# Attention run one stage deeper: scores three steps ahead, maxima two, division by the sums one, values one behind

## The reference

```python
# diff: 4 heads, two score maps each, shared values
a = masked_softmax(s1, mask) - lam * masked_softmax(s2, mask)
out = einsum('bhqk,bkhd->bqhd', a, v)
# fox: 8 heads; c is the cumulated log of the forget gate
s = einsum('bqhd,bkhd->bhqk', qb, k) * scale + cq[..., :, None] - c[..., None, :]
out = einsum('bhqk,bkhd->bqhd', masked_softmax(s, mask), v)
# nsa: 16 heads in 4 groups; compressed, selected and window keys
o = gb[:, :, 0] * o_c + gb[:, :, 1] * o_s + gb[:, :, 2] * o_w
```

## Time and profile before

| | before |
|---|---|
| median of 3 runs | 2183.83 us |
| profiled execution, time | 2185.85 us |
| profiled execution, span from first to last instruction | 2184.0 us |
| mean granted TensorE clock | 0.938 |
| busy: TensorE, VectorE, ScalarE, GpSimd | 1835.5, 638.7, 477.5, 461.3 us |
| attention, first scores to last output copy | 144 to 879 us |
| last fill ends | 787 us |

### The profile page before, as it was taken

The page is one execution under the profiler, slowest core; times in us unless marked ns, Lnnn a source line. Parts: engine busy times, 40 slices in busy tenths (PEclk is TensorE's granted clock), DMA queues, the critical chain, the costliest instruction groups (busy, mean ns, idle before and its releaser), DMA issues. The chain is left out here.

```text
span 2184.0 us, 27742 instructions
## 1 busy us (share of the span) xinstructions
PE 1835.5 (84%) x11130; PEld 1284.6 (59%) x11130; DVE 638.7 (29%) x1270; ACT 477.5 (22%) x1005; POOL 461.3 (21%) x340
## 2 busy tenths in 40 slices
PE   6999999999999977999748878888788888787870
PEld 4887777776666654888635545554455555454530
DVE  4433334436665577100321111111111111111115
ACT  4222323323434343222201010101010101010101
POOL 2333323332221120344121111111111111111100
PEclk9999999999999987999969999999999999999995
DMA  9552222332131120233539999999999999999966
GB/s 266 125 160 77 77 59 78 77 74 52 39 68 49 44 111 1 68 99 95 234 146 421 420 423 421 422 420 423 421 422 421 420 421 422 420 421 418 416 252 249
DMA packets 206614, 527.21 MB, mean 241 GB/s; under 512 B 65922, under 2 KB 149154, under 8 KB 162122
## 3 DMA queue, kind: packets, MB, share of 16 engines
q1 hardware_dynamic: 187738, 509.15, 61.2%
q0 software_dynamic: 18800, 17.00, 2.3%
HBM read 530.38 MB, written 46.03 MB: 264 GB/s over the span
## 5 line engine op out<-in xcount | busy, mean ns | idle before, releaser
L790 PE MATMUL PJ<-ht_rounded,ring_rounded 128*128 128x512 f32 (+1 forms) x928 | 322.7, 401 | 4.5 <-ACT at_region L1148 3.8
L1031 PE MATMUL PJ<-ht_region,ring_region 128*64 128x256 f32 x1024 | 254.7, 412 | 65.7 <-DMA ht_region<-in_w_up 65.7
L1031 PE MATMUL PJ<-at_region,ring_region 128*64 128x256 f32 x1024 | 243.2, 399 | 58.5 <-DMA at_region<-in_w_up 57.6
L1032 PE MATMUL PJ<-ht_region,ring_region 128*64 128x256 f32 x1024 | 255.4, 413 | 0.0
L1032 PE MATMUL PJ<-at_region,ring_region 128*64 128x256 f32 x1024 | 243.9, 399 | 0.0
L1031 PEld LDWEIGHTS PJ<-ht_region,ring_region 128*64 128x64 f32 x1024 | 150.2, 149 | 152.9 <-issue 96.5
L728 POOL DMA_INDIRECT y_scratch<-ring_region,s_idx x64 | 64.6, 1009 | 789.8 <-DVE ring_region L1653 765.2
L1031 PEld LDWEIGHTS PJ<-at_region,ring_region 128*64 128x64 f32 x1024 | 145.1, 144 | 139.9 <-issue 90.0
L676 POOL TENSOR_TENSOR ring_rounded<-ring_region,at_rounded 128x2048 fp32r<-128x2048 f32 (+1 forms) x31 | 139.7, 4505 | 346.3 <-ACT at_rounded L1093 346.3
L676 POOL TENSOR_TENSOR ring_rounded<-ring_region,ring_rounded 128x2048 fp32r<-128x2048 f32 x30 | 137.7, 4591 | 322.6 <-ACT ring_rounded L1093 322.6
L1645 DVE TENSOR_TENSOR ring_region<-ring_region,PJ 64x256 f32<-64x256 f32 x64 | 27.1, 423 | 603.6 <-ACT ring_region L1294 603.6
(11 more groups left out here) (242 smaller groups left out, 2632.7 us busy)
## 6 DMA issues: line engine op xcount, KB each, us to landing
at_region<-in_w_gate SPq DMA_DIRECT2D x32, 2048.0 KB
at_region<-in_w_up SPq DMA_DIRECT2D x32, 2048.0 KB
at_region<-in_w_down SPq DMA_DIRECT2D x32, 2048.0 KB, 22.6
ht_region<-in_w_gate SPq DMA_DIRECT2D x32, 2048.0 KB
ht_region<-in_w_up SPq DMA_DIRECT2D x32, 2048.0 KB
x_region<-in_w_down SPq DMA_DIRECT2D x32, 2048.0 KB
ring_region<-in_w_in SPq DMA_DIRECT2D x36, 1024.0 KB, 5.9
ring_region<-in_w_out SPq DMA_DIRECT2D x16, 1024.0 KB, 5.2
```

Of the source, the lines that this page charges most:

```text
L790: ins = mm(out, w[:, k, 0:width], h[:, k, :], start=k == 0 and i == 0, stop=k == KT - 1 and i == 2)
L1031: mm(GU[0:CAP, 0:D_EXPERT], x, gate[:, j, :], start=j == 0, stop=j == KT - 1)
L1032: ins = mm(GU[CAP:2 * CAP, 0:D_EXPERT], x, up[:, j, :], start=j == 0, stop=j == KT - 1)
```

## The change

`LOOK` becomes 3. TensorE does in step n: first fill, values of n - 1, transposes of n, second fill, scores of n + 3. VectorE does: maximum of n + 2, division of n + 1, copy of n. ScalarE does: what answers to the first fill, output copy of n - 1, copy of n, exponentials of n + 2, what answers to the second fill. As fills now run one step earlier and end one step earlier, unit 1 has only the two fill places of step 0: `fillings()` puts its first tile in the first and all the rest in the second. The tiny multiplication goes: the scaling takes the reciprocal and the gate (or minus lambda) as two per-partition operands of one operation.

```diff
-LOOK = 2
+LOOK = 3
...
         slots = [(n, half) for n in range(lo, hi) for half in range(2)]
-        slots = slots[:-1] if len(slots) > 4 else slots
+        if len(slots) < 4:
+            (n, half), last = slots[0], slots[-1]
+            for i in range(FIRST[g + 1], FIRST[g + 2]):
+                out[n][half].append((i, 0, KT, False))
+                n, half = last
+                if COLUMNS[i][1] == "v":
+                    out[n][half].append((i, KT, KT, True))
+            continue
+        slots = slots[:-1]
...
             for n in range(ALL_STEPS):
                 fill(n, 0)
+                if n >= 1:
+                    values(n - 1)
                 transpose_probs(n)
+                fill(n, 1)
                 if n + LOOK < ALL_STEPS:
                     scores(n + LOOK)
-                fill(n, 1)
-                values(n)
+            values(ALL_STEPS - 1)
...
             exps(0)
+            exps(1)
             for n in range(ALL_STEPS):
-                if n + 1 < ALL_STEPS:
-                    exps(n + 1)
+                after_fill(n, 0)
                 if n >= 1:
                     out_copy(n - 1)
-                after_fill(n, 0)
                 copy_pT(n)
+                if n + 2 < ALL_STEPS:
+                    exps(n + 2)
                 after_fill(n, 1)
...
-                    link(v.tensor_tensor(coef[:, par, 0:1], neglam, rinv[:, par, 1:2], ALU.mult))
-                    link(v.tensor_scalar(p2, p2, coef[:, par, 0:1], None, ALU.mult))
+                    link(v.tensor_scalar(p2, p2, rinv[:, par, 1:2], neglam, ALU.mult, ALU.mult))
...
+                    for half, p in enumerate((p1, p2)):
+                        if kind == "fox":
+                            ins = v.tensor_scalar(p, p, c[:, half:half + 1], None, ALU.mult)
+                        else:
+                            ins = v.tensor_scalar(p, p, c[:, half:half + 1], gates[:, qb, which + half:which + half + 1],
+                                                  ALU.mult, ALU.mult)
...
             for n in range(ALL_STEPS):
                 after_fill(n, 0)
-                copy_pT(n)
+                if n + 2 < ALL_STEPS:
+                    row_max(n + 2)
                 if n + 1 < ALL_STEPS:
                     normalise(n + 1)
-                if n + LOOK < ALL_STEPS:
-                    row_max(n + LOOK)
+                copy_pT(n)
                 after_fill(n, 1)
```

More of the change, by code:

```diff
@@ L382, in hybrid_block_moe_kernel @@
         csum = tiny(2, 2)
-        coef = tiny(2, 2)
         ccoef = tiny(2, 2)
@@ L1489, in normalise @@
                     link(v.reciprocal(c, rsum[:, par, :]))
-                    if kind != "fox":
-                        which = NSA_HEADS * (1 if kind == "slc" else 2) + u * 4 + pr * 2
-                        link(v.tensor_tensor(coef[:, par, :], gates[:, qb, which:which + 2], c, ALU.mult))
-                        c = coef[:, par, :]
-                    v.tensor_scalar(p1, p1, c[:, 0:1], None, ALU.mult)
-                    ins = v.tensor_scalar(p2, p2, c[:, 1:2], None, ALU.mult)
+                    which = NSA_HEADS * (1 if kind == "slc" else 2) + u * 4 + pr * 2
+                    for half, p in enumerate((p1, p2)):
[4 more added lines that the diff above has]
+                                                  ALU.mult, ALU.mult)
                 ins.then_inc(normed, 1)
@@ L1517, in after_fill @@
                         take_out(tile)
-            for n in range(LOOK):
-                row_max(n)
+            row_max(0)
+            row_max(1)
             normalise(0)
```

## The result

The changed kernel took 2195.36 us (median of 7 runs, 2193.47 to 2201.5), the kernel before 2185.15 us on the same chip (7 runs, 2181.47 to 2188.8): a ratio of 1.0058, 95% interval 1.0042 to 1.0073. It is 0.6% slower by this ratio, 10.2 us by the medians, where 2142 us and "faster" were forecast. The profiled execution took 2193.62 us, its span 2191.7.

A forecast was written before the change was run, and what follows sets the result against it. TensorE was taken to bound attention's filled part, a loop of latencies its unfilled end. Terms 27.4 - 0.5 + 16.5 + 1.8 - 3 = 42.2 us off 2185.85 gave 2143.7, predicted as 2142 us, range 2122 to 2168.

The forecast's parts named there:

- I count all 18.9 us of these waits as gone: Filled part of attention: values' waits for ScalarE's copy of the transposed probabilities vanish, 18.9 us gained.
- Removing it does not remove the wait ... I count nothing for it: Tiny multiplications stalled by GpSimd's subtraction: the scalings behind would wait likewise; counted 0, at most 7.0 us in the end.
- Turned v tile, -4 of 7.6, with +1.5 for the exponentials ahead of it: Filled part: ScalarE's earlier take saves 4 of 7.6 us; exponentials ahead add 0.5 us in each of three later nsa units.
- 2.7 + 0.8 us: Step 0, unit 1's three tiles together: 2.7 us added waiting for the turned tile, 0.8 for the q-to-k hand-over.
- Clock, -6: Filled part: with TensorE's idles gone, 6 of the 8.4 us lost to slow clock come back.
- The filled part as a whole, -27.4: Attention while projections fill between its matmuls: 32.4 us gained less 5.0 us added, net 27.4 us.
- Transposes, -3.5: Filled part: transposes' 3.5 us of waits for the division vanish, since division ends a step earlier.
- the extra step in the unfilled part: One more step unfilled (23 instead of 22), paced by VectorE's 3.8 us instead of TensorE's 3.3: +0.5 us.
- -16.5: Unfilled part: VectorE's waits fall by 10.4 us for the exponentials and 6.1 for the transposes, 16.5 us together.
- -3: Unfilled part: 3 us given back to TensorE at 1.2 GHz in steps of one and two key blocks.
- One operation, -1.8: Unfilled part: dropping the tiny multiplication saves 3.6 us, the scalings' second operand costs 1.8; net gain 1.8 us.
- Rival (d): Slower: takes of the second fill wait behind exponentials and maximum in 14 places, 56 us lost, 2198 us; chance 0.03.

The follow-up runs named there:

- e3: Changed kernel with GpSimd's subtractions during attention cut to one of 16 slices, TensorE multiplying high parts instead of low: 2169.6 us, ratio 0.9921.
- e1: Changed kernel with VectorE's copy of the transposed probabilities moved ahead of the division: 2193.6 us, ratio 1.0025.
- Pieces: GpSimd's subtraction issued as 8 instructions of 256 columns instead of one of 2048; ratio 0.9960 on the kernel before, 0.9952 on the changed kernel.
- e6: Kernel before with GpSimd's subtraction issued as 8 instructions instead of one: 2176.4 us, ratio 0.9960.
- e9: Kernel before with the subtraction in 8 instructions and ScalarE's weight rounding after the take of the turned v tile: 2161.7 us, ratio 0.9894.
- e8: Changed kernel with subtraction in 8 instructions, weight rounding after the turned-v take, and VectorE's copy ahead of the division: 2148.8 us, ratio 0.9830.
- e10: As e8, but TensorE issues the scores of step 2 behind the first fill of step 0 instead of ahead of it: 2144.1 us, ratio 0.9813.
- late rounding: ScalarE rounds the second next weight tile after taking the turned v tile, not before; alone on the changed kernel 2178.4 us, ratio 0.9973.
- copy first: VectorE's order maximum, copy, division instead of maximum, division, copy; alone on the changed kernel 2193.6 us, ratio 1.0025.
- e5: Changed kernel with GpSimd's subtraction issued as 8 instructions instead of one: 2174.6 us, ratio 0.9952.
- e7: Changed kernel with ScalarE's rounding of the second next weight tile after the take of the turned v tile: 2178.4 us, ratio 0.9973.

## Why the prediction was wrong

- **"I count all 18.9 us of these waits as gone": the step that failed.** ScalarE's half of the copy is on time, and that wait is 0. But values wait for both halves, and I followed only the one that the trace named. The new order puts VectorE's half behind the division: 21.0 us of new waits, so +2.1 instead of -18.9. 14.4 us of them went with the long subtraction (e3), and in e1, where the copy stands ahead of the division, none is left under that name.
- **"Removing it does not remove the wait ... I count nothing for it": right that the wait stays, wrong that it costs the same.** I had the place before my eyes and the rule with it, and asked only whether the stall goes with the tiny operation. A move past a lock has to ask which instructions fall into its time now, and who waits behind them. Pieces give 0.4% before and 1.1% after the change (ratios 0.9960, and 1.0058 to 0.9952): about 9 and 23 us, so some 14 us of the miss of 53. The Trainium skill ("SBUF — State Buffer", Who interferes with whom) says that between GpSimd and a VectorE operation in a two-port mode whichever issues first gets the shared port pair for its whole instruction and the other fully blocks. The rows agree for GpSimd first (4.94 us with GpSimd 0.30 us ahead); for VectorE first no run here has an overlap of more than 0.10 us.
- **Turned v tile, -4 of 7.6, with +1.5 for the exponentials ahead of it.** It came to 17.4 us. In step 0 the 2.7 + 0.8 us were right (2.92 and 0.69). The places at 462, 534, 637 and 739 us took 2.94, 3.50, 2.07 and 2.07. ScalarE in front of the take was round 1.91, output copy, copy and exponentials 1.3: I had left out the round, which I had counted for step 0. Moving it is worth 18.6 us here by the ratios, but on the kernel before with pieces 14.4 us too (e6 to e9), so that of the miss only some 4 us can be put down to it, which is no more than the intervals leave open.
- **Not seen: scores of step 2.** With three steps of scores ahead of the first fill and two score banks, the third waits for the exponentials of step 0: 2.76 us. What it costs in the time stays open (e8 against e10, above).
- **Clock, -6.** It fell from 0.99 to 0.97 over the filled part. Reckoned as in the prediction, 0.03 x 178 + 0.05 x 280 = 19.3 us go to the lower clock instead of 8.4, so about +11 instead of -6. I took less idle time to mean more clock; there was more of it, and nine waits were of 2.07 to 6.35 us, eight of them followed by half clock.
- **The filled part as a whole, -27.4.** It became 21.9 us longer for the same work (18.6 + 3.3): 14.8 us of idle time and 7.1 of clock. Even with pieces, late rounding and copy first the order is worth nothing there (e9 against e10): it takes 9.5 us off the values' wait and adds as much in waits of its own. The forecast subtracted the first and put the second at 5.0 us.
- **Transposes, -3.5, and the extra step in the unfilled part:** right.
- **Unfilled part.** From 92.8 us my terms (-16.5, -1.8, -3, +3.8 for the added step) lead to 75.3; it took 82.9. VectorE's wait for the exponentials fell from 10.4 to 1.2 us, for the transposes from 11.1 to 6.3, a full period at four key blocks was 3.58 us (875.26 to 878.84), a little under the forecast 3.7 to 3.9, VectorE was 83% busy ("over 85%" was forecast). The missing 7.6 us is about the one wait of 7.25 at 814.45, the lock again: without the long subtraction the part took 74.3 us (e3), with pieces and copy first 74.0 (e8) and 75.8 (e10). The mechanism was right, and one stall of it was left out.
- **One operation, -1.8:** 2.5 measured (0.2 to 4); a pair of 512 columns takes 1.00 us, which is the rate of the scaling with one operand (0.49 each) and not that of the two-tensor add (0.69).
- **Rival (d)** has the right sign and, at 2198, nearly the right number, but by accident: the waits for the turned tile are 10 us longer and not 56, and the largest item in front of them is the round, not the exponentials. Its chance of 0.03 was too small all the same, because all cases shared one assumption, that VectorE's order costs nothing in the filled part. No rival questioned it.

Against the changed kernel the corrections measured alone are, by the ratios, pieces 23, rounding late 19 and copy first 7 us, and all three together 50: they add up. (By the medians it is 20.8, 17.0, 2 and 46.6, and copy first 8.1 us behind the other two; that it gains by their company is therefore not shown.) The fastest version, e10, took 2144.1 us, 1.9% below the kernel before. Of its 41 us, 23.5 come without the deeper order. So the order freed of what stood in its way gains 12.9 to 17.6 us with the one operation in it, all of it in the unfilled part, where 42.2 were forecast.

## What to carry to other kernels

A wait is released by the last of its conditions, and the profile names the last one of before; when an order changes, follow every condition, above all the ones that were never named. Where two engines share a lock, list which instructions fall into the long holder's time before and after, and cut the long instruction before moving anything. Look at the longest wait of a group as well as at its sum: behind eight of the nine longest in the filled part of the changed kernel TensorE ran at half clock for a while. Before a difference between two profiled executions is credited to an edit, see that it does not lie ahead of the place where the edit acts (4.5 us here between e8 and e10).

## What the runs showed of the hardware

- Two scalings (SBUF to SBUF, 512 columns) that begin after a GpSimd subtraction of 4.5 us end 0.75 us after it; with the subtraction in eight pieces they are held 0.57 us (604.37) and 0.90 us (608.52, both in e5). The eight pieces take 5.5 to 6.5 us in all instead of 4.5 to 4.8, as in e8:

```profile
589.92 5.93 POOL L684 TENSOR_TENSOR ring_rounded<-ring_region,at_rounded 128x256 fp32r<-128x256 f32 x8 [19.01 <-ACT at_rounded L1107]
```

- VectorE's copy out of PSUM (0.68 us, e1 at 608.45) and bias add with one operand in SBUF and one in PSUM (0.69 us, before at 598.29) took their usual time while the subtraction ran.
- TensorE's clock, over the filled parts of before and changed kernel: of the waits up to 1.99 us three (1.31, 1.77 and 1.31 us long) were followed by some us at 1.2 GHz, of the nine from 2.07 us on eight were. Length alone does not decide: behind the wait of 2.77 us in e7 (151.25) and of 2.76 in e8 (152.18) the clock stayed at 1.00. What else decides, no run here settles.
